# Layer norms as two VectorE passes with stores by halves, the first up weights in buffers of their own, and another order at the first norm

## What is computed

```python
proj = h @ w_in                              # 1024 x 4888
q, k_c, v_c, k_s, v_s, k_w, v_w, nsa_gl, u, v, merge_gl = split(proj)
o_nsa = native_sparse_attention(...)         # compressed, selected and window branches
o_sgu = spatial_gating(u, v, ...)
merged = g_nsa * (o_nsa @ w_branch_nsa) + g_sgu * (o_sgu @ w_branch_sgu)
mix = merged @ w_out
h = layer_norm(ALPHA * h + mix, ln1_g, ln1_b)
ffn = (silu(h @ w_ffn_gate) * (h @ w_ffn_up)) @ w_ffn_down      # hidden width 2816
h = layer_norm(ALPHA * h + ffn, ln2_g, ln2_b)

def layer_norm(x, g, b):
    mu = mean(x); var = mean(square(x - mu))
    return (x - mu) * rsqrt(var + 1e-5) * g + b
```

## Time and profile before

| what | value |
|---|---|
| time, median of 3 runs | 756.57 us (756.43 to 756.87) |
| the profiled execution's own time | 755.22 us |
| its span | 753.1 us |
| PE busy | 733.6 us (97%) |
| DVE busy | 379.3 us (50%) |
| ACT busy | 306.2 us (41%) |
| POOL busy | 114.8 us (15%) |
| mean granted PE clock | 0.995 |

### The profile page before, as it was taken

The page is one execution under the profiler, slowest core; times in us unless marked ns, Lnnn a source line. Parts: engine busy times, 40 slices in busy tenths (PEclk is TensorE's granted clock), DMA queues, the critical chain, the costliest instruction groups (busy, mean ns, idle before and its releaser), DMA issues.

```text
span 753.1 us, 9672 instructions
## 1 busy us (share of the span) xinstructions
PE 733.6 (97%) x3709; PEld 619.5 (82%) x3709; DVE 379.3 (50%) x651; ACT 306.2 (41%) x467; POOL 114.8 (15%) x134
## 2 busy tenths in 40 slices
PE   7999999999999999999999999999999999999994
PEld 6889887888888988888789888888888888888883
DVE  3523287797778784664973312322332243233575
ACT  3513476567767777332343222332232132213511
POOL 2507090523343430000110000000000000000011
PEclk9999999999999999999999999999999999999998
DMA  8424233112101205536313233223313321332202
GB/s 260 154 87 163 61 104 121 57 37 77 55 2 57 57 1 141 195 112 223 112 57 96 72 111 111 65 102 111 111 61 106 111 100 68 112 111 90 77 29 84
DMA packets 57167, 72.73 MB, mean 97 GB/s; under 512 B 3856, under 2 KB 44336, under 8 KB 57136
## 3 DMA queue, kind: packets, MB, share of 16 engines
q1 hardware_dynamic: 57136, 72.32, 29.4%
HBM read 70.21 MB, written 2.10 MB: 96 GB/s over the span
## 4 chain that ended last, share of the span: by engine, by line
PE 89%; DVE 6%; ACT 2%; issue 2%; DMA 1%; POOLq 0%; POOL 0%; SPq 0%; ACTq 0%; DVEq 0%
PE ps L1280 79%; PE ps L1292 4%; PE ps L1288 3%; PE ps L1289 3%; DVE stat L1164 1%; DVE y L1189 1%; DVE wl L885 1%; DMA arena<-in_x 1%; ACT y L826 1%; DVE prob L1102 1%; ACT wh L596 1%; DVE ptl L895 0%; DVE y L1192 0%; DVE y L1169 0%; DVE wl L895 0%
## 5 line engine op out<-in xcount | busy, mean ns | idle before, releaser
L885 DVE TENSOR_TENSOR wl<-stage,wh 128x2048 fp32r<-128x2048 f32 (+1 forms) x49 | 111.8, 2282 | 206.8 <-ACT wh L602 177.7
L1280 PE MATMUL ps<-wh,xh 128*128 128x512 f32 (+1 forms) x384 | 148.6, 387 | 0.0
L1280 PE MATMUL ps<-wh,xl 128*128 128x512 f32 (+1 forms) x384 | 146.8, 382 | 0.0
L1280 PE MATMUL ps<-wl,xh 128*128 128x512 f32 (+1 forms) x384 | 146.7, 382 | 0.0
L1280 PE MATMUL ps<-ath,wh 128*128 128x512 f32 (+1 forms) x384 | 146.1, 380 | 0.0
L1280 PE MATMUL ps<-atl,wh 128*128 128x512 f32 (+1 forms) x384 | 146.0, 380 | 0.0
L1280 PE MATMUL ps<-ath,wl 128*128 128x512 f32 (+1 forms) x384 | 146.0, 380 | 0.0
L602 ACT CAST wh<-stage 128x2048 fp32r<-128x2048 f32 x37 | 70.5, 1906 | 166.4 <-PE ps L1280 166.4
L1280 PEld LDWEIGHTS ps<-wh,xl 128*128 128x128 f32 x384 | 72.3, 188 | 14.1
L1280 PEld LDWEIGHTS ps<-wh,xh 128*128 128x128 f32 x384 | 72.4, 189 | 13.6 <-DVE wl L885 0.3
L1280 PEld LDWEIGHTS ps<-ath,wh 128*128 128x128 f32 x384 | 72.2, 188 | 13.8
(11 more groups left out here) (238 smaller groups left out, 1028.8 us busy)
## 6 DMA issues: line engine op xcount, KB each, us to landing
stage<-in_w_in SPq DMA_DIRECT2D x28, 512.0 KB, 4.5
stage<-in_w_ffn_gate SPq DMA_DIRECT2D x22, 512.0 KB, 4.4
stage<-in_w_ffn_up SPq DMA_DIRECT2D x22, 512.0 KB, 4.5
stage<-in_w_ffn_down SPq DMA_DIRECT2D x22, 512.0 KB, 3.8
stage<-in_w_out SPq DMA_DIRECT2D x8, 512.0 KB, 4.5
arena<-in_x SPq DMA_DIRECT2D x8, 256.0 KB, 5.9
stage<-in_w_in SPq DMA_DIRECT2D x8, 256.0 KB, 6.2
stage<-in_w_branch_nsa SPq DMA_DIRECT2D x4, 512.0 KB, 7.5
```

The lines of the kernel that those rows point to most:

```text
L885: dve.tensor_tensor(wl[:, slot, 0:n], stage[slot][:, 0:n], wh[:, slot, 0:n].bitcast(fp32), ALU.subtract).then_inc(w_lo, 1)
L1280: return pe.matmul(out, (sh, sh, sl)[i], (mh, ml, mh)[i], start=start and i == 0, stop=stop and i == 2)
```

## The change

It has four parts. The norm becomes two DVE passes: (y - mean) * gain in four quarters of 256 columns, with the four one-column operations of the reciprocal root between them, and then y * root + bias in two halves of 512, each of which counts its own `h_ok`. ACT's mean subtraction and POOL's bias are gone. The last block is stored in two halves. The first up unit gets `second_h` and `second_l`: ACT writes the high part after its first root, and POOL writes the low part. The statistics of the first column half follow each `add_rows`, and `ht_lo_of(0)` and `ht_lo_of(1)` move.

```diff
@@ buffers @@
-        sb("fact_before", [P, FT - 8, SEQ], fp32, early)
+        sb("fact_before", [P, FT - 16, SEQ], fp32, early)
+        second_h = sb("second_h", [P, 2048], f32r, early)
+        second_l = sb("second_l", [P, 2048], f32r, early)
@@ sync: the stores @@
-            for m in range(MT):
+            for m in range(MT - 1):
                 for h in h_ok:
                     sp.wait_ge(h, MT + m + 1)
                 sp.dma_start(out_d[:, m, :], y[:, m, :]).then_inc(stored, 16)
-            sp.wait_ge(stored, 16 * MT)
+            m = MT - 1
+            for half in range(2):
+                c = slice(512 * half, 512 * half + 512)
+                sp.wait_ge(h_ok[half], MT + m + 1)
+                sp.dma_start(out_d[:, m, c], y[:, m, c]).then_inc(stored, 16)
+            sp.wait_ge(stored, 16 * (MT + 1))
@@ gpsimd @@
-            for k in range(2 * MT):
-                ln, m = divmod(k, MT)
-                pool.wait_ge(scaled, k + 1)
-                pool.tensor_tensor(y[:, m, BIAS_COLS:D], y[:, m, BIAS_COLS:D], lnb[:, ln, BIAS_COLS:D],
-                                   ALU.add).then_inc(h_ok[1], 1)
+            pool.wait_ge(w_hi, U_FFN + 2)
+            pool.wait_ge(w_lo, U_FFN + 1)
+            pool.tensor_tensor(second_l[:, :], stage[1][:, :], second_h[:, :].bitcast(fp32),
+                               ALU.subtract).then_inc(w_lo, 1)
@@ scalar @@
                 act.activation(nrm[:, m, 1:2], nrm[:, m, 0:1], ACT.Sqrt).then_inc(sq_ok, 1)
-                act.activation(y[:, m, :], y[:, m, :], ACT.Identity, bias=nrm[:, m, 4:5]).then_inc(centred, 1)
...
             root(0)
+            split_to(second_h[:, :], U_FFN + 1, 1, U_BRANCH)
             root(1)
             ht_hi_of(0)
+            ht_hi_of(1)
             root(2)
-            ht_hi_of(1)
-            late_split(U_FFN + 1, 1)
+            ht_hi_of(2)
             root(3)
-            ht_hi_of(2)
             ht_hi_of(3)
@@ vector: norm(k) @@
-                n = nrm[:, m, :]
+                v, root, r, t = [nrm[:, m, c:c + 1] for c in range(4)]
+
+                def centre(quarter):
+                    c = slice(256 * quarter, 256 * quarter + 256)
+                    step.later(dve.scalar_tensor_tensor(out=y[:, m, c], in0=y[:, m, c], scalar=mv[:, m, 0:1],
+                                                        in1=lng[:, ln, c], op0=ALU.subtract, op1=ALU.mult))
+
+                centre(0)
                 dve.wait_ge(sq_ok, k + 1)
...
+                step.later(dve.reciprocal(r, root))
+                at = step.n
+                centre(1)
+                dve.wait_ge(dve_step, at)
+                step.later(dve.scalar_tensor_tensor(out=t, in0=r, scalar=v, in1=r, op0=ALU.mult, op1=ALU.mult))
...
+                step(dve.tensor_tensor(t, t, r, ALU.mult))
+                for half in range(2):
+                    c = slice(512 * half, 512 * half + 512)
+                    dve.scalar_tensor_tensor(out=y[:, m, c], in0=y[:, m, c], scalar=t, in1=lnb[:, ln, c],
+                                             op0=ALU.mult, op1=ALU.add).then_inc(h_ok[half], 1)
@@ vector: the first norm @@
                 add_rows(m, 0, m).then_inc(mg_lo, 1)
+                dve.wait_ge(mg_lo, KD + m + 1)
+                moments(m, 0)
             split(U_OUT + 3, 1)
-            dve.wait_ge(mg_lo, KD + MT)
-            for m in range(MT):
-                moments(m, 0)
             split_to(first_l[:, :], first_h[:, :], U_FFN, 0)
...
                 if m == 2:
+                    ht_lo_of(1)
+                norm(m)
+                if m == 1:
                     ht_lo_of(0)
-                    ht_lo_of(1)
-                if m == 3:
-                    split(U_FFN + 1, 1)
-                norm(m)
             ht_lo_of(2)
             ht_lo_of(3)
+            dve.wait_ge(w_lo, U_FFN + 2)
@@ tensor @@
-            views = [tuple(t[:, :].rearrange("p (k n) -> p k n", k=8) for t in (first_h, first_l)),
-                     (w8(wh, 1), w8(wl, 1))]
+            views = [tuple(t[:, :].rearrange("p (k n) -> p k n", k=8) for t in pair)
+                     for pair in ((first_h, first_l), (second_h, second_l))]
```

More of the change, by code:

```diff
@@ L77, in build_layer @@
     FILL_FIRST = 2
-    BIAS_COLS = 704
     x_d = T["x"][0].rearrange("(m p) c -> p m c", p=P)
@@ L322, in build_layer @@
         x2_arrived, ln_arrived = sem("x2_arrived"), sem("ln_arrived")
-        var_ok, sq_ok, centred, scaled = sem("var_ok"), sem("sq_ok"), sem("centred"), sem("scaled")
+        var_ok, sq_ok = sem("var_ok"), sem("sq_ok")
         h_ok = [sem("h_ok0"), sem("h_ok1")]
@@ L366, in __init__, with later, __call__ @@
                 self.eng, self.s, self.n = eng, s, 0
-            def __call__(self, ins):
+            def later(self, ins):
                 ins.then_inc(self.s, 1)
                 self.n = self.n + 1
+            def __call__(self, ins):
+                self.later(ins)
                 self.eng.wait_ge(self.s, self.n)
@@ L1170, in add_rows, with variance @@
                                                 op1=ALU.add)
-            def variance(m):
-                step(dve.bn_aggr(mv[:, m, :], stat[:, m, :, :].rearrange("p a b -> p (a b)")))
-                dve.tensor_scalar(nrm[:, m, 4:5], mv[:, m, 0:1], -1.0, None, ALU.mult)
+            def variance(m, groups=None):
+                groups = stat[:, m, :, :] if groups is None else groups
+                step(dve.bn_aggr(mv[:, m, :], groups.rearrange("p a b -> p (a b)")))
                 dve.tensor_scalar(nrm[:, m, 0:1], mv[:, m, 1:2], EPS, None, ALU.add).then_inc(var_ok, 1)
@@ L1180, in norm @@
                 ln, m = divmod(k, MT)
-                n = nrm[:, m, :]
-                dve.wait_ge(sq_ok, k + 1)
[L1183 to L1193, removed]
+                v, root, r, t = [nrm[:, m, c:c + 1] for c in range(4)]
@@ new lines, in norm @@
+                dve.wait_ge(dve_step, at)
+                step.later(dve.scalar_tensor_tensor(out=t, in0=r, scalar=v, in1=r, op0=ALU.mult, op1=ALU.mult))
+                at = step.n
+                centre(2)
+                dve.wait_ge(dve_step, at)
+                step.later(dve.tensor_scalar(t, t, -0.5, 1.5, ALU.mult, ALU.add))
+                at = step.n
+                centre(3)
+                dve.wait_ge(dve_step, at)
+                step(dve.tensor_tensor(t, t, r, ALU.mult))
[3 more added lines that the diff above has]
+                                             op0=ALU.mult, op1=ALU.add).then_inc(h_ok[half], 1)
```

## The result

The changed kernel takes **758.27 us** (median of 9 runs, 757.80 to 759.08), the kernel before 756.43 (median of 9, 755.32 to 756.87). The ratio is 1.003, with a 95% interval of 1.0021 to 1.0039: it is slower, by 1.6 to 3.0 us. The forecast was 754.9 and faster. The time lies in the stated range, and the profile is that of the first rival (758.5).

The account below looks back on a forecast made before the run. PE, busy 97% of the span, bounds the kernel; only its first-norm waits (2.8 us) and the tail can be won. First norm -0.2 and tail -1.5 give -1.7: 756.57 to 754.9 us, range 752.9 to 758.4.

Parts of the forecast that it names:

- the first rival: First norm: POOL's split gets in ahead of a half of block 0; waits 5.0 against 2.8; 758.5 or 757.3; chance 0.24.
- The price of the norm: Each block's norm: 3.6 us from variance to the end of the second half against 4.54 before, 1.0 less (0.4 to 1.5).
- Block 0's sum: First norm: with statistics moved earlier, DVE starts it at 363.27, not 363.90; block 0 ready in time, wait of 1.6 goes.
- The tail: After PE's last matmul: 1.0 us from the norm plus 0.55 from the stores, together -1.5 us (-0.4 to -2.8).
- the part of the half stores: Last block: second 256 KB store lands 2.05 us after issue, against 2.6 for the whole 512 KB: 0.55 won.
- POOL's subtraction: First up unit's low part, 2048 columns on POOL: 4.6 us by extrapolation (bounds 2.3 and 5.8).
- The mechanism read from the earlier trace: DVE operations with two SBUF inputs don't run while POOL's does: a DVE split at 139.96 took 2.70 instead of 2.28 us.
- Who gets in first?: First norm: DVE's second half of block 0 precedes waiting POOL, which starts at 368.5 and holds DVE until about 372.95.
- POOL's scaling of 1.75 us at 164.74: Earlier-trace row behind the order taken: needing 0.70 us alone, it took 1.75 because DVE's follower went ahead of waiting POOL.
- the clock: After a long PE wait at block 0 the clock may fall: some six matmuls losing 0.2 us each, 1.2 us.
- The thin margin: POOL may start at 367.3, block 0's first half ends at 367.1: only 0.2 us against POOL catching the moment before it.
- the case that it described: POOL works after block 0's second half; PE waits 1.5, 0.4 and 0.7 us afterwards; 754.9 us; chance 0.5.

Follow-up runs that it names:

- run 1: The change, with POOL's subtraction also waiting until block 0's second half is done: 753.39 us, ratio 0.9957 to the kernel before.
- run 2: The change, with POOL's subtraction also waiting for block 1's second half: 751.36 us, ratio 0.9929 to the kernel before.
- run 3: The change, with POOL writing zeros to second_l by memset instead of subtracting, reading nothing from SBUF: 751.34 us, ratio 0.9938 to the kernel before.
- run 4: The change, with eighteen matmuls of unused result on PE ahead of block 0's transposes: 756.04 us, ratio 0.9994 to the kernel before.
- run 7: The change, with POOL's subtraction cut into four operations of 512 columns at the old place: 752.56 us, ratio 0.9955 to the kernel before.
- run 8: The change, with the norm's second pass as one instruction of 1024 columns at the first norm: 752.27 us, ratio 0.9951 to the kernel before.
- run 9: The change, with the norm's second pass in four instructions of 256 columns at both norms: 758.52 us in a single run, beside 756.17 before.
- run 10: The change, with the last block stored whole as before: 758.30 us, ratio 1.0031 to the kernel before.
- run 5: The kernel before with only the two-pass norm, old order and whole last store: 753.40 us, ratio 0.9966 to the kernel before.
- run 6: The change, with DVE writing second_l ahead of block 3's norm and POOL not splitting: 751.37 us, ratio 0.9934 to the kernel before.

## Why the prediction was wrong

**What held.** PE is bounded by its own work, and only the first norm and the tail could move: so it was in all runs. The price of the norm (3.6 us from the variance to the second half) is 3.5 in run 1 (365.29 to 368.80). Block 0's sum comes as soon as PE has the rows, as forecast, and without the collision PE doesn't wait there (runs 1 to 3). The tail gives 1.62 us (1.5 forecast) in the trace; the part of the half stores, 0.6, is in the trace alone. POOL's subtraction takes 4.60 (4.6 from the extrapolation of the earlier trace rows). The mechanism read from the earlier trace rows, that two-input passes don't run beside POOL's, holds in the change and in runs 1, 4, 7, 8, 9 and 10 without exception, and run 3 narrows it to POOL's reads.

**The step that failed** is "Who gets in first?", with its sentence "DVE's follower went ahead of the waiting POOL. I take this: POOL starts its data at 368.5, after block 0's second half". It rested on one row, POOL's scaling of 1.75 us at 164.74. The runs show the opposite five times: in the change, in runs 7 and 9, in run 4 (second half held, POOL 5.04) and in run 10 (second half held, POOL 4.95), POOL began while a two-input pass of DVE was running, and had the ports at that pass's end, though DVE's next pass followed without a wait. The Trainium skill's rule ("SBUF — State Buffer", section on who interferes with whom), that whoever issues first gets the pair for the whole instruction, agrees with this: POOL at 368.99 came before the second half at 369.48. I had set a single row against it. That row had a rival reading which I did not price: POOL began there 0.14 us before DVE's next instruction, against 0.22 in run 9, 0.49 in run 7 and in the change, and may not yet have been asking for the ports. No run tests this. Against it as a general rule, POOL's two-input operation at 62.78 in the trace before went ahead of a split of DVE with 0.08 us in hand (2.81 us instead of 2.28, with DVE idle before it). At 164.74 the operation (a scaling) and DVE's running instruction (L1060, one tensor input) are of other kinds, so why DVE won there stays open.

The same trace also held a handover like the one that came, with the engines exchanged, in the stretch of the earlier trace rows. DVE stood from 139.96 behind POOL's 139.78. POOL's next operation followed without a wait at 140.45, and it was this one that stood: 2.46 us, against 0.40 for the shortest of its kind. The engine that had waited went ahead of the other's follower. I had not weighed this.

```profile
62.78 0.75 POOL L512 TENSOR_TENSOR pcmp<-arena,trig 128x256 f32<-128x256 f32 x1
62.86 2.81 DVE L885 TENSOR_TENSOR wl<-stage,wh 128x2048 fp32r<-128x2048 f32 x1 [5.54 <-ACT wh L596]
...
140.45 2.46 POOL L564 CAST vs<-arena 128x256 fp32r<-128x256 f32 x1
```

The consequence was priced in the first rival with the right sign: waits of 5.0 in place of 2.8 (measured 4.8 in place of 3.3 start to start, 4.5 in place of 2.8 by the rows' idle time), a tail of -1.5 (-1.62), and the clock. Two terms there were mis-sized. The waits grew by 1.5 us, not 2.2. The clock cost 2.6 us in the rows and 2.2 between the medians, not 1.2: the estimate had six matmuls that lose 0.2 each, and there were eight transposes that lost 0.77 together and nine matmuls that lost 1.8. Against the rival's sum the waits were 0.7 less, the clock 1.4 more, and 0.7 came back behind the norm. These cancel, so that 758.5 against 758.27 is partly luck.

**The chances.** "The thin margin" was noticed and then not used. The forecast of 754.9 is also off for the case that it described: that case is run 1, with 753.4. It has 3.0 us less than the kernel before, where the forecast had 1.7. By the traces the waits fell by 0.5 us start to start (3.3 to 2.8) instead of 0.2, the tail by 1.6 instead of 1.5, and the stretch from block 3's transposes to the second iteration took 20.15 us instead of 20.86, for which the forecast had no term. Run 1 is faster than the kernel before and the change slower, and one POOL instruction's place separates them.

**Where the gain went.** Without the collision the change gives -5.0 us (run 2): -2.9 for the norm (run 5), and 2.1 for the order, the up unit's own buffers and the half stores (0.6 of it by the trace of run 10). The collision takes 4.7 of it back with the clock held up (756.04 - 751.36, run 4 against run 2), the lower clock another 2.2.

## What to carry to other kernels

Before work is moved to GpSimd, list DVE's two-input SBUF passes that lie within its duration and ask who waits for each. One GpSimd instruction that reads SBUF holds the first of them that comes after a boundary for its whole length, however early DVE's chain had begun: so order it by a semaphore behind the last pass that counts, or cut it into short pieces, and cut DVE's own pass no finer than is needed while GpSimd waits. And a stop of TensorE of 4 us is to be priced with the matmuls that run at half clock behind it, here half of the wait once more.

## What I had not expected of the hardware

- **Matmuls of 256 columns come at two rates.** From block 3's transposes on, in the first feed-forward iteration, they start 0.113 us apart in some profiles (the change, runs 1, 6 and 8) and 0.118 or more in the others, all at the full granted clock. From block 3's transposes to the second iteration's first silu it is 20.16 us in the change and 20.86 before, so this gives up to 0.7 us back. How long PE had waited doesn't explain it: run 10 and run 9 wait as long as the change and have 20.67, and run 6 waits least of the fast four. Nor does PE's program: that of run 10 is the change's. Each kernel has one profile, so whether the rate belongs to a kernel or to an execution isn't known, nor is its cause. The rows of the two, the change first, then run 2:

```profile
400.74 0.28 PE L1299 MATMUL ps<-ath,first_h 128*128 128x256 f32 x1
400.85 0.28 PE L1299 MATMUL ps<-atl,first_h 128*128 128x256 f32 x1
400.97 0.28 PE L1299 MATMUL ps<-ath,first_l 128*128 128x256 f32 x1
```

```profile
401.89 0.28 PE L1300 MATMUL ps<-ath,second_l 128*128 128x256 f32 x1
402.01 0.28 PE L1300 MATMUL ps<-ath,second_h 128*128 128x256 f32 x1
402.13 0.28 PE L1300 MATMUL ps<-atl,second_h 128*128 128x256 f32 x1
```

- **A shown duration of POOL can include waiting for the ports**, and that is how the order is read: 4.60 alone, 4.95 in the change, 5.57 behind a pass of 1024 columns.
- **Filling PE's gap with useless matmuls is worth 2.2 us** here: they keep the granted clock at 1.00 over 369 to 374 us, where the change has 0.85 and then 0.50.
